# A rearranged opening of a hybrid encoder layer, with 27 products of a constant on TensorE

## The chip, the cores and the metric

The kernel runs on one core of a Trainium2 chip. The metric is the device time of one execution in microseconds; a kernel is given by the median of its runs. The engines of the core are called PE (TensorE, matrix products), DVE (VectorE), ACT (ScalarE), POOL (GpSimd) and SP (SyncE, which here issues the DMAs). A core has one queue of instructions for each engine; they meet only at semaphores. SBUF holds 128 partitions, and products are written to eight banks of PSUM.

## What is computed

One layer of a streaming encoder, in float32, for a prompt of 1024 frames and a sample of 64 frames, so 1088 token rows of width 1024:

```python
def _rmsnorm(x, g):
    y = x * lax.rsqrt(jnp.mean(x * x, axis=-1, keepdims=True) + EPS)
    return y * g

def _swiglu_half(x, g, w_gate, w_up, w_down):        # w_gate, w_up: 1024 x 2816
    h = _rmsnorm(x, g)
    return 0.5 * ((jax.nn.silu(h @ w_gate) * (h @ w_up)) @ w_down)

x = x + _swiglu_half(x, g_ffn1, w1_gate, w1_up, w1_down)
x = x + mix(x)                  # attention and mLSTM heads, in and out projections
x = x + _swiglu_half(x, g_ffn2, w2_gate, w2_up, w2_down)
x = _rmsnorm(x, g_final)
```

The change lies in the first 40 us or so, in the norm of the first `_swiglu_half` and in the first of its gate and up products.

## The kernel before

**Precision and products.** A float32 product is made of three passes (`three_pass`, lines 291 to 293): each operand is split into a high part (ACT copies it to a rounded type) and a low part (a subtraction, operand less its high part), and TensorE sums high x low, high x high and low x high. The up and gate products of the FFN go in pairs of 128-column tiles of the weights, 11 pairs in all; from the second pair on, the pair is done with seven products in place of eight (Strassen's scheme), on sums of operand quarters. The first pair, "the opening", is done directly, as 16 chains of 24 products with 272 columns each (`start_chain`), a chain for each matrix (gate, then up), token half j, and quarter i.

**The opening.** x comes in nine blocks of 128 rows (the ninth, block 8, has the 64 rows of the sample) by DMA to XIN. For each block TensorE transposes eight squares into two banks (line 845), and DVE (line 856) or ACT (line 851) copies the two banks to X. ACT squares the rows with an accumulated sum (line 862) and takes roots in groups of blocks (`GROUP`, line 869); DVE makes reciprocals (line 874) and diagonal matrices of them (line 877); TensorE multiplies ONES with these diagonals (line 888, `start_roots`, n = 0 to 3), which puts 1/rms of every token into a bank across all partitions. DVE scales X with it and with the gain (line 935, `start_scale`), ACT makes the high part (line 946), DVE the low part (line 950). The four weight quarters of the gate and the four of the up matrix get their high parts on ACT (line 961) and their low parts on DVE (line 965).

**The second token half and the spill.** The unscaled X is needed later for the residual, so SP writes it to DRAM as soon as all of it has been copied out of PSUM (`xsp`, line 465, four DMAs: two for the first half of the tokens, then two for the second half). The scale of the first half writes to a buffer of its own (HJ); the scale of the second half writes in place into X and therefore waits until the DMA of that part has landed. The wait of SP before the second pair of DMAs is `sp.wait_ge(x_evA, 10)`: ACT's tenth copy, which is the second bank of block 8.

**What sets the order.** Everything around the change is written out by hand, one list of calls for each engine: `start_pe_tokens`, `start_pe_pair`, `start_act_tokens`, `start_dve_tokens`. An engine goes through its list and stands still at a wait that isn't fulfilled. Behind the opening, `start_difference` and `start_feature` steps (lines 1020, 1035, 1042) make the operand sums of the token quarters for the seven products, and `up` steps make those of the weights: sums on GpSimd (lines 556, 558, 559, 566), high parts on ACT (line 578), low parts on DVE (line 583); lines 703, 765 and 768 add up products on DVE and GpSimd.

## Time and profile before

| what | value |
|---|---|
| time, median of 3 runs | 1945.61 us (1944.47 to 1946.06) |
| the profiled execution | 1945.54 us, of which the span of the trace 1944.0 us |
| mean granted TensorE clock in it | 0.998 |
| TensorE busy | 1924.2 us (99%) |
| VectorE, ScalarE, GpSimd busy | 66%, 40%, 54% |
| DMA, mean | 151 GB/s |

Where a row of a timeline has "x4", four instructions one behind the other are joined, and the duration is that of all; the bracket at the end says how long the engine was idle before, and who ended that idle time.

### The profile page before, as it was taken

What the parts mean: (1) busy time and instruction counts of PE and PEld (TensorE: products, weight loads), DVE (VectorE), ACT (ScalarE), POOL (GpSimd) and SP (SyncE); (2) the same over time, 40 slices, a digit from 0 to 9 for tenths busy, and PEclk for the clock granted to TensorE, in tenths of its full rate; (3) what the DMA queues carried; (4) which work ended last, traced back from release to release, by engine and by line L of the source; (5) the groups of instructions that cost most, each with busy time, mean ns of one, the idle gap of its engine ahead of it and who ended that gap; (6) DMA issues with size and microseconds to landing.
All of it is one profiled execution on the core that took longest, in us unless ns stands there. A gap on an engine that the chain in (4) does not pass through costs nothing.

```text
span 1944.0 us, 39225 instructions
## 1 busy us (share of the span) xinstructions
PE 1924.2 (99%) x14627; PEld 1882.3 (97%) x14627; DVE 1284.3 (66%) x1882; ACT 783.4 (40%) x1595; POOL 1053.3 (54%) x958
## 2 busy tenths in 40 slices
PE   8999999999999999999999999999999999999998
PEld 7999999999999999999998999999999999999997
DVE  6866777666566788864445664866767667656674
ACT  6433333333443345733334542443333333344343
POOL 2277776775777641321222442237767776686770
PEclk9999999999999999999999999999999999999999
DMA  8135445334986530342332834214454444498552
GB/s 271 46 114 178 140 162 179 132 132 156 316 311 188 169 102 14 116 119 90 100 104 62 207 94 124 79 56 145 150 180 144 132 154 164 151 362 276 165 157 104
DMA packets 226846, 293.88 MB, mean 151 GB/s; under 512 B 16616, under 2 KB 158472, under 8 KB 226736
## 3 DMA queue, kind: packets, MB, share of 16 engines
q1 hardware_dynamic: 219040, 272.76, 43.8%
q0 software_dynamic: 7696, 19.63, 3.2%
q8 instruction: 71, 1.16, 0.3%
q14 instruction: 39, 0.32, 0.1%
HBM read 198.07 MB, written 94.21 MB: 150 GB/s over the span
## 4 chain that ended last, share of the span: by engine, by line
PE 96%; DVE 1%; DMA 1%; issue 1%; POOL 1%; ACT 0%; SPq 0%; ACTq 0%; POOLq 0%
PE bank L291 29%; PE bank L292 29%; PE bank L293 29%; PE bank L2583 1%; PE bank L2602 1%; PE bank L2593 1%; DMA XIN<-in_x_prompt 1%; PE bank L2514 0%; PE bank L1332 0%; PE bank L1334 0%; PE bank L1333 0%; PE bank L1328 0%; PE bank L845 0%; PE bank L2694 0%; PE bank L2692 0%
## 5 line engine op out<-in xcount | busy, mean ns | idle before, releaser
L291 PE MATMUL bank<-HA,HW 128*128 128x272 f32 x1120 | 322.7, 288 | 0.0
L292 PE MATMUL bank<-HA,HW 128*128 128x272 f32 x1120 | 322.3, 288 | 0.0
L293 PE MATMUL bank<-HA,HW 128*128 128x272 f32 x1120 | 322.1, 288 | 0.0
L1381 DVE SCALAR_TENSOR_TENSOR HW<-WRAW,HW 128x512 fp32r<-128x512 f32 x140 | 224.5, 1644 | 103.8 <-ACT HW L1376 103.3
L1387 POOL TENSOR_TENSOR HA<-ARAW,HA 128x544 fp32r<-128x544 f32 x140 | 222.6, 1607 | 101.8 <-ACT HA L1375 101.6
L291 PE MATMUL bank<-HL,WGH 128*128 128x368 f32 (+2 forms) x784 | 255.6, 326 | 0.0
L293 PE MATMUL bank<-HH,WGL 128*128 128x368 f32 (+2 forms) x784 | 246.3, 314 | 1.1 <-issue 1.1
L292 PE MATMUL bank<-HH,WGH 128*128 128x368 f32 (+2 forms) x784 | 246.2, 314 | 0.0
L292 PE MATMUL bank<-FC,WR 128*128 128x272 f32 x768 | 222.1, 289 | 0.0
L291 PE MATMUL bank<-FC,WR 128*128 128x272 f32 x768 | 220.4, 287 | 0.6 <-DVE WR L583 0.5
L293 PE MATMUL bank<-FC,WR 128*128 128x272 f32 x768 | 220.1, 287 | 0.0
L292 PEld LDWEIGHTS bank<-HA,HW 128*128 128x128 f32 x1120 | 211.1, 189 | 0.0
L293 PEld LDWEIGHTS bank<-HA,HW 128*128 128x128 f32 x1120 | 211.1, 189 | 0.0
L291 PEld LDWEIGHTS bank<-HA,HW 128*128 128x128 f32 x1120 | 210.5, 188 | 0.2 <-POOL HA L1387 0.2
L814 POOL TENSOR_TENSOR SA<-SA,PV 128x272 f32<-128x272 f32 x160 | 140.4, 898 | 101.3 <-DVE PV L703 98.1
L583 DVE TENSOR_TENSOR WR<-RAWU,WR 128x512 fp32r<-128x512 f32 x100 | 99.3, 993 | 134.3 <-ACT WR L578 134.3
L1375 ACT ACTIVATE HA<-ARAW 128x544 fp32r<-128x544 f32 x140 | 91.6, 654 | 232.3 <-PE bank L293 163.5
L629 ACT ACTIVATE SA<-SA 128x272 f32<-128x272 f32 x160 | 67.5, 431 | 265.9 <-POOL SA L768 137.0
L703 DVE TENSOR_TENSOR PV<-bank,PV 128x272 f32<-128x272 f32 x280 | 118.5, 435 | 77.6 <-POOL PV L765 38.5
L291 PEld LDWEIGHTS bank<-HL,WGH 128*128 128x128 f32 x784 | 147.3, 188 | 14.6 <-issue 12.9
L292 PEld LDWEIGHTS bank<-HH,WGH 128*128 128x128 f32 x784 | 147.5, 188 | 1.6
L293 PEld LDWEIGHTS bank<-HH,WGL 128*128 128x128 f32 x784 | 147.4, 188 | 1.0 <-issue 1.0
(384 smaller groups left out, 5670.6 us busy)
## 6 DMA issues: line engine op xcount, KB each, us to landing
asp<-SA SPq DMA_DIRECT2D x44, 544.0 KB, 3.5
RAWG<-in_w_gate SPq DMA_DIRECT2D x22, 1024.0 KB, 6.5
RAWU<-in_w_up SPq DMA_DIRECT2D x22, 1024.0 KB, 6.4
tsp<-TT SPq DMA_DIRECT2D x40, 544.0 KB, 6.6
ARAW<-tsp SPq DMA_DIRECT2D x80, 272.0 KB, 3.4
WS<-in_w_down SPq DMA_DIRECT2D x20, 1024.0 KB, 8.6
wsp<-WS SPq DMA_DIRECT2D x20, 1024.0 KB, 8.6
WRAW<-wsp SPq DMA_DIRECT2D x80, 256.0 KB, 4.3
```

The source lines that it names most:

```text
L291: nc.tensor.matmul(bank[:, 0:w], w_hi, rhs_lo, start=first, stop=False)
L292: nc.tensor.matmul(bank[:, 0:w], w_hi, rhs_hi, start=False, stop=False)
L293: return nc.tensor.matmul(bank[:, 0:w], w_lo, rhs_hi, start=False, stop=last)
L583: nc.vector.tensor_tensor(WR[:, o, 1], weight(o, q0, mat), WR[:, o, 0].bitcast(F32), ALU.subtract).then_inc(s_.lo, 1)
L629: nc.scalar.activation(tile, tile, ACT.Silu).then_inc(s_.silu, 1)
L703: nc.vector.tensor_tensor(out, bank, add, ALU.add).then_inc(s_.ev, 1)
L814: nc.gpsimd.tensor_tensor(gated(j, slot), gated(j, slot), PV[j][:, tile], ALU.mult).then_inc(s_.mul, 1)
L1375: nc.scalar.activation(HA[f][h][:, 0], ARAW[r][:, :, :], ACT.Copy).then_inc(down_hi, 1)
L1381: nc.vector.scalar_tensor_tensor(out=HW[f][h][:, 1], in0=WRAW[r][:, :], scalar=0.5, in1=HW[f][h][:, 0].bitcast(F32), op0=ALU.mult, op1=ALU ...
L1387: nc.gpsimd.tensor_tensor(HA[f][h][:, 1], ARAW[r][:, :, :], HA[f][h][:, 0].bitcast(F32), ALU.subtract).then_inc(down_alo, 1)
L2583: mm = nc.tensor.matmul(BANK[2 + i // 2][:, (i % 2) * 256:(i % 2) * 256 + 256], QB[rows, par, 2 * g_ + hl // 2, :], KW[rows, par, 0 if g_ ...
L2593: tr = nc.tensor.transpose(BANK[4 + w][:, i * P:(i + 1) * P], SP[:, i, w * P:(w + 1) * P], IDENT[:, :])
```

## The change

It rewrites the four lists of the opening and what hangs on their counts.

- GpSimd makes ONES first, then issues the DMA of the gain and makes the other constants. Behind its constants it computes the low parts of the eight weight quarters (`start_weight_low_pool`), which DVE did.
- TensorE waits for ONES alone, multiplies ONES by ONES 8 times into bank 7, which nothing reads, and then for the other constants. Five such products stand between the transposes of block 1 and block 2, three ahead of the first roots and eleven behind them, 27 in all (`start_idle`). Only blocks 0 to 4 are transposed ahead of the first chain (before: 0 to 5); block 5 and the second roots follow behind it, and the third and fourth roots one chain later than before.
- The roots come in five groups (before: four), blocks 0 and 1 apart from block 2; all later counts of the semaphores follow (`ROOTS`).
- DVE copies blocks 0, 1, the first bank of 2, then 3 and 4; ACT the second bank of 2, then 5 to 8. So ACT makes 9 copies and DVE 9.
- ACT's list: weight quarters 4 to 7 and the squares of blocks 5, 6 and 7 stand ahead of the copy of block 8.
- The banks of the opening's chains rotate over six banks instead of using four; a chain waits for whoever last used its bank (`start_bank_free`). A chain of the first token half waits for the low parts of its two weight quarters one by one.
- SP's wait ahead of the spill of the second half is again for the second bank of block 8 (now ACT's ninth copy).

```diff
-        GROUP = ((0, 3, P), (3, 5, P), (5, 8, P), (8, 9, DEC))
+        GROUP = ((0, 2, P), (2, 3, P), (3, 5, P), (5, 8, P), (8, 9, DEC))
+        ROOTS = len(GROUP)
...
             elif j:
-                sp.wait_ge(x_evA, 10)
+                sp.wait_ge(x_evA, 9)
             else:
-                sp.wait_ge(x_evV, 8)
-                sp.wait_ge(x_evA, 4)
+                sp.wait_ge(x_evV, 9)
+                sp.wait_ge(x_evA, 1)
...
-        BLOCK_BANK = (0, 2, 4, 6, 2, 0, 6, 2, 6)
+        BLOCK_BANK = (0, 2, 4, 6, 2, 6, 2, 6, 6)
...
+        def start_weight_low_pool(pool, i):
+            pool.wait_ge(st.whi, i + 1)
+            nc.gpsimd.tensor_tensor(WR[:, i, 1], first_weight(i), WR[:, i, 0].bitcast(F32), ALU.subtract).then_inc(st.wlo, 1)
...
+        def start_bank(f, mat, j, i):
+            return BANK[i if f else (8 * j + 4 * mat + i) % 6]
...
         def start_chain(pe, f, mat, j, i, between=None):
             fh, th = (i // 2, i % 2) if mat and j else (i % 2, i // 2)
             if j == 0:
-                pe.wait_ge(st.wlo, 8 * f + 4 * mat + 2 * fh + 2)
-            if mat:
+                pe.wait_ge(st.wlo, 8 * f + 4 * mat + 2 * fh + (2 if f else 1))
+            if f == 0:
+                start_bank_free(pe, mat, j, i)
+            elif mat:
...
             for kh in range(2):
                 e = 2 * th + kh
+                if f == 0 and j == 0 and kh:
+                    pe.wait_ge(st.wlo, 4 * mat + 2 * fh + 2)
...
+        def start_idle(pe, count):
+            for _ in range(count):
+                nc.tensor.matmul(BANK[7][:, 0:P], ONES[:, :], ONES[:, :], start=True, stop=True)
+
         def start_pe_tokens(pe):
-            for b in range(3):
-                start_transpose(pe, b)
+            pe.wait_ge(const_ops, 1)
+            start_idle(pe, 8)
+            pe.wait_ge(const_ops, 7)
+            start_transpose(pe, 0)
+            start_transpose(pe, 1)
+            start_idle(pe, 5)
+            start_transpose(pe, 2)
+            start_idle(pe, 3)
             start_roots(pe, 0)
-            for b in range(3, 6):
-                start_transpose(pe, b)
-            start_roots(pe, 1)
+            start_idle(pe, 11)
+            start_transpose(pe, 3)
+            start_transpose(pe, 4)
...
                 start_chain(pe, f, 0, 0, 0)
+                start_transpose(pe, 5)
+                start_roots(pe, 1)
                 start_transpose(pe, 6)
+                start_chain(pe, f, 0, 0, 1)
                 start_transpose(pe, 7)
-                start_chain(pe, f, 0, 0, 1)
+                start_chain(pe, f, 0, 0, 2)
                 start_transpose(pe, 8)
-                start_chain(pe, f, 0, 0, 2)
-                start_chain(pe, f, 0, 0, 3, between=lambda: start_roots(pe, 2))
+                start_chain(pe, f, 0, 0, 3)
+                start_chain(pe, f, 1, 0, 0, between=lambda: start_roots(pe, 2))
                 start_roots(pe, 3)
...
+            for i in range(8):
+                start_weight_low_pool(pool, i)
             up_pool(pool, 0)
```

**ACT, between the weight quarters 2 and 3 and the end of its list.** The names: XIN is x as loaded, X x transposed, HJ x scaled, FC and FBa operands of the products, WR the split weights, RAWG and RAWU the loaded ones, JK and SSB squares and their sums, RMB roots, DG diagonals. L961 are weight high parts, L851 copies from PSUM (4x128: a bank of a full block; 4x64: a bank of block 8), L946 high parts of the scaled x, L862 squares, L869 (L867 now) roots. Before:

```order
L862 ACTIVATE JK,SSB<-XIN_78 128x1024
L851 ACTIVATE X<-bank 128x4x128 x2
L946 ACTIVATE FBa<-HJ_65 128x4x272
L851 ACTIVATE X<-bank 128x4x128 x2
L946 ACTIVATE FC<-HJ_65 128x4x272
L961 ACTIVATE WR<-RAWU 128x512 x2
L862 ACTIVATE JK,SSB<-XIN_78 128x1024 x2
L869 ACTIVATE RMB<-SSB,GQOE 128x3
L851 ACTIVATE X<-bank 128x4x64 x2
```

The same place of ACT's queue after the change:

```order
L851 ACTIVATE X<-bank 128x4x128 x4
L946 ACTIVATE FBa<-HJ_65 128x4x272
L946 ACTIVATE FC<-HJ_65 128x4x272
L851 ACTIVATE X<-bank 128x4x128 x2
L961 ACTIVATE WR<-RAWU 128x512 x4
L862 ACTIVATE JK,SSB<-XIN_78 128x1024 x3
L867 ACTIVATE RMB<-SSB,GQOE 128x3
L851 ACTIVATE X<-bank 128x4x64 x2
```

Between the copy of block 7 and that of block 8 (4x64) now stand four weight high parts, three squares and a root; before, one x high part, two weight high parts, two squares and a root stood there.

**DVE, from the first diagonals to the second scale.** L856 are copies from PSUM, L874 (L872 now) reciprocals, L877 (L875) diagonals, L935 scales, L950 low parts of x, L965 low parts of the weights. Before:

```order
L856 COPY X<-bank 128x4x128 x6
L874 RECIPROCAL RMB<-RMB 128x3
L877 TENSOR_SCALAR DG<-IDENT,RMB 128x128 x3
L935 SCALAR_TENSOR_TENSOR HJ_65<-X,GC,bank 128x272 x8
L950 TENSOR_TENSOR FC<-HJ_65,FC 128x4x272
L874 RECIPROCAL RMB<-RMB 128x2
L877 TENSOR_SCALAR DG<-IDENT,RMB 128x128 x2
L965 TENSOR_TENSOR WR<-RAWG,WR 128x512 x2
L950 TENSOR_TENSOR FBa<-HJ_65,FBa 128x4x272
```

DVE's queue at that place after the change:

```order
L856 COPY X<-bank 128x4x128
L872 RECIPROCAL RMB<-RMB 128x1
L875 TENSOR_SCALAR DG<-IDENT,RMB 128x128
L935 SCALAR_TENSOR_TENSOR HJ_65<-X,GC,bank 128x272 x8
L950 TENSOR_TENSOR FC<-HJ_65,FC 128x4x272
L950 TENSOR_TENSOR FBa<-HJ_65,FBa 128x4x272
L856 COPY X<-bank 128x4x128 x2
```

The weight low parts are gone from DVE, one copy and one diagonal stand between block 2's first bank and the first scale instead of two copies and three diagonals, and the two low parts of x follow one another.

## Rows read from the trace of the kernel before

**Rows 1.** The page's first part: busy time, share of the span, instructions.
```profile
PE 1924.2 (99%) x14627; PEld 1882.3 (97%) x14627; DVE 1284.3 (66%) x1882; ACT 783.4 (40%) x1595; POOL 1053.3 (54%) x958
```

**Rows 2.** TensorE's waits, 0 to 110 us: total us, times, longest.
```profile
PE bank L845 <- POOL BD L1699: 5.1, 1, 5.1
...
PE bank L291 <- DVE WR L583: 0.5, 1, 0.5
```

**Rows 3.** Timeline of TensorE, opening: start, duration, operation, [idle before <-releaser].
```profile
5.05 3.65 PE L845 MATMUL bank<-IDENT,XIN 128*128 128x128 f32 x16 [5.05 <-POOL BD L1699]
...
12.12 0.84 PE L888 MATMUL bank<-DG,ONES 128*128 128x128 f32 x6 [1.74 <-DVE DG L877]
14.61 5.38 PE L845 MATMUL bank<-IDENT,XIN 128*128 128x128 f32 x24 [1.65 <-DMA XIN<-in_x_prompt]
...
20.73 0.36 PE L291 MATMUL bank<-FC,WR 128*128 128x272 f32 x1
...
21.94 0.28 PE L291 MATMUL bank<-FC,WR 128*128 128x272 f32 x1
```

**Rows 4.** Timeline of DVE, 40 to 102 us.
```profile
40.95 1.72 DVE L935 SCALAR_TENSOR_TENSOR X<-X,GC,bank 128x272 f32<-128x272 f32 x4 [1.96 <-DMA xsp<-X]
...
65.91 2.25 DVE L583 TENSOR_TENSOR WR<-SS,WR 128x512 fp32r<-128x512 f32 x2
...
72.99 1.28 DVE L583 TENSOR_TENSOR WR<-RAWG,WR 128x512 fp32r<-128x512 f32 x2
...
74.54 1.43 DVE L583 TENSOR_TENSOR WR<-RAWG,WR 128x512 fp32r<-128x512 f32 x1
...
76.42 1.65 DVE L1042 TENSOR_TENSOR FBa<-TS,FBa 128x1088 fp32r<-128x1088 f32 x1
78.11 2.26 DVE L1020 TENSOR_TENSOR TS<-X,TS 128x1088 f32<-128x1088 f32 x1
...
100.45 1.39 DVE L583 TENSOR_TENSOR WR<-RAWU,WR 128x512 fp32r<-128x512 f32 x1 [1.02 <-ACT WR L578]
```

**Rows 5.** The waits of SP's queue, 0 to 60 us: total us, times, longest.
```profile
SPq L465 <- ACT X L851: 9.3, 1, 9.3
```

**Rows 6.** Timeline of ACT, 26 to 33 us.
```profile
26.41 1.09 ACT L851 ACTIVATE X<-bank 128x512 f32<-128x512 f32 x2
27.36 1.14 ACT L946 ACTIVATE FC<-HJ 128x1088 fp32r<-128x1088 f32 x1
28.37 1.17 ACT L961 ACTIVATE WR<-RAWU 128x512 fp32r<-128x512 f32 x2
29.41 1.08 ACT L862 ACTIVATE JK<-XIN 128x1024 f32<-128x1024 f32 x1
...
31.85 0.30 ACT L869 ACTIVATE RMB<-SSB,GQOE 128x3 f32<-128x3 f32 x1
32.05 0.64 ACT L851 ACTIVATE X<-bank 128x256 f32<-128x256 f32 x2
```

**Rows 7.** Windows: stretch, length, busy time of each engine, PEclk, DMA share, GB/s.
```profile
14.00:16.00 2.00, 1.39 (x7) 1.39 (x8) 2.00 (x6) 2.00 (x5) 0.00 (x0) 0.50 1.09 352
...
20.00:22.00 2.00, 1.87 (x16) 1.79 (x16) 2.00 (x4) 1.97 (x4) 0.00 (x0) 1.00 1.13 226
```

**Rows 8.** Timeline of DVE, 9 to 19 us.
```profile
9.98 1.29 DVE L856 COPY X<-bank 128x512 f32<-128x512 f32 x2 [0.55 <-PE bank L845]
...
11.39 0.68 DVE L877 TENSOR_SCALAR DG<-IDENT,RMB 128x128 f32<-128x128 f32 x3
13.07 3.36 DVE L935 SCALAR_TENSOR_TENSOR HJ<-X,GC,bank 128x272 f32<-128x272 f32 x8 [1.00 <-issue]
16.77 1.29 DVE L950 TENSOR_TENSOR FC<-HJ,FC 128x1088 fp32r<-128x1088 f32 x1 [0.34 <-ACT FC L946]
```

**Rows 9.** Timeline of POOL (GpSimd), 60 to 80 us.
```profile
65.72 1.28 POOL L566 TENSOR_TENSOR RAWG<-RAWG,SS 128x512 f32<-128x512 f32 x1 [16.30 <-DVE WR L583]
73.18 2.24 POOL L556 TENSOR_TENSOR SS<-RAWU 128x512 f32<-128x512 f32 x1 [6.17 <-PE bank L293]
```

More of the change, by code:

```diff
@@ L838, in start_transpose @@
             pe.wait_ge(block_in[b], 16)
[L839 to L842 removed]
+            if b in (4, 5, 6):
+                pe.wait_ge(x_evV, {4: 4, 5: 7, 6: 9}[b])
+            elif b in (7, 8):
+                pe.wait_ge(x_evA, {7: 3, 8: 7}[b])
             for half in range(2):
@@ L846, in start_transpose, with start_evict_act, start_evict_dve @@
                 tr.then_inc(x_tr, 1)
-        def start_evict_act(act, b):
-            for half in range(2):
+        def start_evict_act(act, b, halves=(0, 1)):
+            for half in halves:
                 act.wait_ge(x_tr, 2 * b + half + 1)
                 nc.scalar.activation(X[:, 4 * half:4 * half + 4, b * P:b * P + (P if b < NB else DEC)], block_banks(b, half), ACT.Copy).then_inc(x_evA, 1)
-        def start_evict_dve(dve, b):
-            for half in range(2):
+        def start_evict_dve(dve, b, halves=(0, 1)):
+            for half in halves:
                 dve.wait_ge(x_tr, 2 * b + half + 1)
@@ L882, in start_roots @@
             if n == 0:
-                pe.wait_ge(x_evV, 6)
-            elif n == 2:
-                pe.wait_ge(x_evA, 10)
+                pe.wait_ge(x_evV, 5)
+            elif n == 1:
+                pe.wait_ge(x_evA, 1)
+            else:
+                pe.wait_ge(x_evA, 9)
             for b, c0, c1 in pieces(n):
@@ L965, in start_weight_low, with start_bank_free @@
             nc.vector.tensor_tensor(WR[:, i, 1], first_weight(i), WR[:, i, 0].bitcast(F32), ALU.subtract).then_inc(st.wlo, 1)
+        def start_bank(f, mat, j, i):
+            return BANK[i if f else (8 * j + 4 * mat + i) % 6]
+        def start_bank_free(pe, mat, j, i):
+            q = 8 * j + 4 * mat + i
+            if q < 2:
+                pe.wait_ge(x_evV, 2)
+            elif q < 4:
+                pe.wait_ge(x_evA, 5)
+            elif q < 6:
+                pe.wait_ge(st.ht, 2 * i + 2)
+            elif q in (10, 11, 12, 13):
+                pe.wait_ge(st.mul, q - 9)
+            else:
+                pe.wait_ge(st.silu, {6: 1, 7: 2, 8: 3, 9: 4, 14: 5, 15: 6}[q])
         def start_chain(pe, f, mat, j, i, between=None):
@@ L994, in start_silu @@
             act.wait_ge(st.pm, 16 * f + 8 * j + i + 1)
-            nc.scalar.activation(gated(j, i % 2 * 2 + i // 2), BANK[i][:, 0:HT], ACT.Silu).then_inc(st.silu, 1)
+            nc.scalar.activation(gated(j, i % 2 * 2 + i // 2), start_bank(f, 0, j, i)[:, 0:HT], ACT.Silu).then_inc(st.silu, 1)
         def start_gate(dve, f, j, i):
@@ L1072, in start_act_tokens @@
         def start_act_tokens(act):
-            for b in range(3):
-                start_block_square(act, b)
+            start_block_square(act, 0)
+            start_block_square(act, 1)
             start_block_root(act, 0)
+            start_block_square(act, 2)
+            start_block_root(act, 1)
+            start_evict_act(act, 2, (1,))
+            start_high(act, 0, 0, 0)
             start_weight_high(act, 0, 0)
+            start_high(act, 0, 0, 1)
             start_weight_high(act, 0, 1)
             start_block_square(act, 3)
-            start_high(act, 0, 0, 0)
             start_block_square(act, 4)
-            start_block_root(act, 1)
-            start_high(act, 0, 0, 1)
-            start_evict_act(act, 5)
-            start_evict_act(act, 3)
+            start_block_root(act, 2)
             start_weight_high(act, 0, 2)
             start_weight_high(act, 0, 3)
-            start_block_square(act, 5)
+            start_evict_act(act, 5)
             start_evict_act(act, 6)
             start_high(act, 0, 0, 2)
+            start_high(act, 0, 0, 3)
             start_evict_act(act, 7)
-            start_high(act, 0, 0, 3)
-            start_weight_high(act, 0, 4)
-            start_weight_high(act, 0, 5)
-            start_block_square(act, 6)
-            start_block_square(act, 7)
-            start_block_root(act, 2)
+            for i in range(4, 8):
+                start_weight_high(act, 0, i)
+            for b in (5, 6, 7):
+                start_block_square(act, b)
+            start_block_root(act, 3)
             start_evict_act(act, 8)
             start_block_square(act, 8)
-            start_block_root(act, 3)
-            start_weight_high(act, 0, 6)
-            start_weight_high(act, 0, 7)
+            start_block_root(act, 4)
         def start_act_features(act):
@@ L1136, in start_dve_tokens @@
         def start_dve_tokens(dve):
-            for b in range(3):
-                start_evict_dve(dve, b)
+            start_evict_dve(dve, 0)
+            start_evict_dve(dve, 1)
             start_diagonals(dve, 0)
+            start_evict_dve(dve, 2, (0,))
+            start_diagonals(dve, 1)
             start_scale(dve, 0, 0, 0, 0)
@@ L1679, in _ @@
         def _(pool):
+            nc.gpsimd.memset(ONES[:, :], 1.0).then_inc(const_ops, 1)
             pool.dma_start(GC[:, 0, :], a["g_ffn1"][0].rearrange("(k p) -> p k", p=P)).then_inc(gain_in, 16)
             nc.gpsimd.memset(IDENT[:, :], 0.0).then_inc(const_ops, 1)
-            nc.gpsimd.memset(ONES[:, :], 1.0).then_inc(const_ops, 1)
             nc.gpsimd.memset(BD[:, :], 0.0).then_inc(const_ops, 1)
```

60 lines of the change are left out of this document (22 added, 38 removed).

## The prediction

> **What bounds the kernel now.** I read the page's busy shares first. TensorE is busy 99% of the span [rows 1], so a microsecond is won or lost only where TensorE waits. Next came the view of what each engine waited for, for TensorE in the first 110 us: 5.1 us until the constants (the row names the last of them) and the first block of x are there, others among the transposes, and then one single wait of 0.5 us, for a DVE subtract of the up weights, in the first Strassen pair [rows 2]. Between the first real matmul at 20.73 [rows 3] and that wait at 101.9, TensorE never stands still. That looks as if the opening were paid only by TensorE. It is not so, and this is the point of the forecast.
>
> Follow the wait backwards on DVE. The subtract that TensorE waited for is the one that starts at 100.45. From there back to 40.95, no DVE row has an idle time that TensorE ended: DVE is full, or waits for ACT or GpSimd, which wait for DVE in turn. The start of this run of work is the scale of the second token half, in place in X, at 40.95, and what it waited for is the landing of the copy of X to DRAM [rows 4]. That copy may only be issued when the last block of x has been copied out of PSUM: SyncE sat 9.3 us until an ACT copy of X [rows 5], the 256-element copy of block 8 at 32.05, which ended at 32.69 [rows 6]. So the time to about 102 us is set by this chain: **ACT's copy of block 8, the spill, DVE's 60 us of operands**, and TensorE's 0.5 us wait shows that TensorE is just ahead of it. Whatever moves block 8's copy moves the end; what makes TensorE start earlier in the opening only lengthens the wait at 102.
>
> **The idle matmuls and the early constant.** The constant's memset moves ahead of one DMA issue and one memset on GpSimd, and the first idle matmuls run before 5.05, when TensorE has nothing [rows 3]. I cost both at nothing; the 5.05 us wait for x covers them. The first broadcast, 272 columns, took 0.84 us [rows 3], so a 128-column product of the same constant is at most 0.84 x 128 / 272 = 0.4 us. Five of them ahead of block 2 are 2.0 us at most. In the old trace the first 16 transposes took 3.65 us, 0.23 each, and the 24 at 14.61 also 0.22 each, in a stretch whose granted clock is 0.50 [rows 3, 7]; so the first ones ran at the lower level (1.2 GHz) as well. If the idle work lifts the clock for them, they are limited by the arrival of block 1, end about 1.7 us earlier, near 7.0, and the five idle ones end at 9.0. Block 2 is there by then and not much sooner: DVE could copy its first half at 9.98 [rows 8], four transposes of 0.23 after 9.06. Eleven behind the broadcast fill the gap to block 3 at 14.61. Without the lift the cover is gone; that is a rival below.
>
> **The first scale** comes earlier. Between the first half of block 2 and the broadcast, DVE had two copies (1.29), a reciprocal and three diagonals (0.68), 9.98 to 12.07, or 2.09 together [rows 8]. Now one copy (half of 1.29), the reciprocal (the 0.12 between) and one diagonal (0.23) stand there, 1.0: the second half goes to ACT, which has time then. The scale starts at 13.07 - 1.1 = 12.0 and ends at 12.0 + 3.36 = 15.4 [rows 8].
>
> **The weight subtracts** go from DVE to GpSimd. DVE saves eight. On GpSimd a subtract of that size took 1.28 us [rows 9]. The first weight is split by ACT after the first activation: 13.7 + 1.1 + 0.6 = 15.4; the second after the second activation: 15.4 + 1.1 + 0.55 = 17.0. Were GpSimd undisturbed, its second subtract would end at 18.3. But in the same 15.4 to 18 DVE now has two subtracts of 1088 columns, 1.29 each [rows 8], with both operands in SBUF. The trace has this case. DVE's pair of 512-column subtracts took 1.28 at 72.99 but 2.25 at 65.91 [rows 4], where GpSimd's 1.28 at 65.72 lay beside it [rows 9]; and the GpSimd sum at 73.18 took 2.24 [rows 9], while DVE's operations at 74.54, 76.42 and 78.11 took 1.43, 1.65 and 2.26 instead of 0.64, 1.29 and 1.29 [rows 4, 8]. The one waits until the other is done. The four operations then come one behind the other: 15.4 + 2 x 1.29 + 2 x 1.28 = 20.5. I take this end, since four rows of the same shapes show it; the other end is 18.3.
>
> (The Trainium skill, GPSIMD Engine Reference, § 1 Specifications, says that GpSimd's SBUF interface is shared with VectorE, and that a VectorE instruction with two SBUF inputs contends. This speaks against moving the subtracts here, and the rows at 65.72 and 65.91 agree with it: 0.97 us more on DVE. By the rule the second subtract ends at 20.5, without it at 18.3, and the sum below is 3.2 or 1.0.)
>
> **From the second subtract to block 8's copy.** The second half of chain 0 needs it: its 12 products, at nine steps from 20.73 to 21.94 [rows 3], are 1.6, so chain 0 ends at 22.1. Only behind it stand block 5's transposes, 0.9 (a third of 5.38, halved for the full clock, which the rows from 20 on show [rows 3, 7]), and the second broadcast with its step to DVE, 0.95 as at 12.12 to 13.07 [rows 3, 8]: the second scale starts at 23.95 and, at 3.36 as the first, ends at 27.3. Then comes ACT's queue, in the new order, where I use the distance from one start to the next in its old rows [rows 6]: activation of the last quarter 1.0, block 7's copies 0.95, four weight splits 2.1 (2 x 1.04), three squares 3.65 (two from 29.41 to 31.85), a root 0.2, block 8's copy 0.64. That sums to 8.55, so the copy ends at 27.3 + 8.55 = 35.85, say 35.9. **It ended at 32.69, so the spill goes out 3.2 us later.** Before, two of those weight splits stood behind the copy, and the last three squares were partly done earlier.
>
> **The sum.** Behind the spill the work is what it was: same landing (issued with the same reload traffic behind it), same DVE and ACT operations. The scale starts at 40.95 + 3.2 = 44.15, the subtract of the up weights ends 3.2 later, and TensorE's wait of 0.5 grows by that and by its own lead. The rest of the 1945.54 profiled us is TensorE's. 1945.54 + 3.2 = **1948.7 us**. The profiled execution and the median of the three runs (1945.61) differ by 0.07, nothing beside the bounds. If the chain came earlier instead, no more than 0.5 us could be won up to 102.
>
> **Rivals.** (a) *The engines do not hold each other up here.* The subtracts end at 18.3, everything from the second half of chain 0 on comes 2.2 us earlier, the shift is 1.0: 1946.5. For it: the operations may interleave otherwise than at 65.72. Against: all rows of like shapes.
> (b) *The opening order does what its start promises*: ACT reaches block 8's copy no later than before, since it takes its squares in gaps that I gave to waiting. Then the old 0.5 us wait is all that can move: 1945.0 to 1945.5. Against: ACT has 2.3 us more of weight splits ahead of the copy than before, whatever the gaps.
> (c) **Slower by more:** *GpSimd's three sums fall differently.* They are released by TensorE (6.17 us idle before 73.18, ended by a TensorE bank [rows 9]), which is about 1 us ahead, while DVE's chain is 3.2 behind; so they lie some 4 us earlier against DVE's work, on operand subtracts. Three sums are 3.9 us; DVE paid 0.75 + 0.36 + 0.97 = 2.1 for them [rows 4]. If it pays all three in full: 1.8 more, 1950.5. It decides from 0.7 us more than forecast. Against: a part of the sums may as well fall on rows where DVE waits for ACT, and then the price falls by as much.
> (d) *The idle matmuls do not do what they say*: the clock stays at 1.2 GHz. Then the first transposes end at 8.7, five idle products 2.0 later, block 2's first four transposes end at 11.6, the scale starts at 13.9 instead of 12.0, and all behind it shifts by 1.9: 1950.6. In the old trace the clock was at 0.50 from 14 to 16, behind a gap that TensorE spent waiting (1.74 and 1.65 us ahead of 12.12 and 14.61 [rows 3]), and at 1.00 from 20 [rows 7], after the transposes had filled it; idle work in just those gaps speaks against this.
>
> **How the numbers follow.** Forecast 0.35, (a) 0.2, (b) 0.13, (c) 0.21, (d) 0.08, and 0.03 for something that gains by a way I don't see. A difference under 0.2%, 3.9 us, can hardly be told from no change here: the bounds are 1941.7 and 1949.5. Forecast, (a) and (b) lie inside, (c) and (d) outside; of the forecast a small part, 0.03, lies beyond the bound. Faster 0.03, same 0.65, slower 0.32. The range reaches from the middle of (b), 1945.2, to beyond (c), 1951.0, which leaves out about 0.07 + 0.03 below and 0.06 above.
>
> **What will show it.** Right: block 8's copy ends near 35.9 on ACT; DVE's scale after the spill starts near 44.2; the single TensorE wait before 110 us for an up-weight subtract has grown to some 4 us or has split into several; the first subtracts on GpSimd or DVE's beside them are longer than 1.29. Wrong: a copy of block 8 at 33 or earlier, or TensorE dense to 102 although the scale is late. The granted clock from 12 to 20 at 1.00 would show the idle work's effect, and a first chain that still waits for its weights shows that it wins nothing by it.

## The result and the profile after the change

The changed kernel takes 1948.78 us (median of 16 runs, 1947.8 to 1951.17) against 1945.08 for the kernel before, measured with it (16 runs): a ratio of 1.0021, with a 95% interval of 1.0014 to 1.0028. It is slower by about 4 us (3.7 between the medians), and 1948.7 was forecast. The profiled execution took 1947.88 (span 1946.3), near the lowest of the 16.

What TensorE waited for between its first chain and 112 us (total, times, longest), where before it was 0.5 us for an up-weight subtract [rows 2]:

```profile
PE bank L291 <- DVE SA L1023: 3.9, 1, 3.9
```

One wait of 3.9 us, eight times the old one, but for another instruction: the product of gate and up (L1023, L1002 before), the third of the opening's second token half. It reads the bank which TensorE's third Strassen product writes next; until then that product waits.

The timeline of ACT, where the chain was expected to be late (start, duration, operation, [idle before <-releaser]); it answers to [rows 6]:

```profile
26.40 1.12 ACT L946 ACTIVATE FC<-HJ 128x1088 fp32r<-128x1088 f32 x1 [0.52 <-DVE HJ L935]
27.42 1.07 ACT L851 ACTIVATE X<-bank 128x512 f32<-128x512 f32 x2
28.37 2.19 ACT L961 ACTIVATE WR<-RAWU 128x512 fp32r<-128x512 f32 x4
30.45 1.05 ACT L862 ACTIVATE JK<-XIN 128x1024 f32<-128x1024 f32 x1
...
34.32 0.64 ACT L851 ACTIVATE X<-bank 128x256 f32<-128x256 f32 x2
```

The last high part, block 7's copies, four weight splits, three squares (the first at 30.45), a root, and only then block 8's copy, which ends at 34.96: 2.27 us later than before. In these two profiles the whole delay arises here: ACT begins this stretch at 26.40, as it did before (26.41, there with block 7's copies [rows 6]), and the stretch has two weight splits more (1.04) and one square more (1.24). Then DVE, in the opening (answering to [rows 8]) and behind the spill (to [rows 4]):

```profile
12.02 3.36 DVE L935 SCALAR_TENSOR_TENSOR HJ<-X,GC,bank 128x272 f32<-128x272 f32 x8 [1.01 <-PE bank L888]
...
16.55 2.12 DVE L950 TENSOR_TENSOR FBa<-HJ,FBa 128x1088 fp32r<-128x1088 f32 x1
...
23.01 3.36 DVE L935 SCALAR_TENSOR_TENSOR HJ<-X,GC,bank 128x272 f32<-128x272 f32 x8 [1.35 <-ACT X L851]
...
43.23 1.78 DVE L935 SCALAR_TENSOR_TENSOR X<-X,GC,bank 128x272 f32<-128x272 f32 x4 [2.03 <-DMA xsp<-X]
...
46.48 2.17 DVE L950 TENSOR_TENSOR FBa<-X,FBa 128x1088 fp32r<-128x1088 f32 x1
...
72.56 2.33 DVE L1041 TENSOR_TENSOR TS<-X,TS 128x1088 f32<-128x1088 f32 x1
74.81 1.58 DVE L585 TENSOR_TENSOR WR<-RAWG,WR 128x512 fp32r<-128x512 f32 x1
76.32 2.35 DVE L1041 TENSOR_TENSOR TS<-X 128x1088 f32<-128x1088 f32 x1
78.59 0.42 DVE L1023 TENSOR_TENSOR SA<-SA,bank 128x272 f32<-128x272 f32 x1
...
104.12 1.39 DVE L585 TENSOR_TENSOR WR<-RAWU,WR 128x512 fp32r<-128x512 f32 x1 [1.02 <-ACT WR L580]
```

The scale behind the spill starts at 43.23 instead of 40.95 (+2.28), the up-weight subtract at 104.12 instead of 100.45 (+3.67). In between, four operations are 0.9 to 1.1 us longer than their like: 46.48 (2.17 for 1.28), 72.56, 74.81 (1.58 for 0.68) and 76.32, the last three directly ahead of the product at 78.59 that TensorE waits for. GpSimd shows why (answering to [rows 9]):

```profile
15.49 4.13 POOL L965 TENSOR_TENSOR WR<-RAWG,WR 128x512 fp32r<-128x512 f32 x2 [3.04 <-ACT WR L961]
...
47.57 2.22 POOL L560 TENSOR_TENSOR SS<-SS,RAWG 128x512 f32<-128x512 f32 x1
...
72.44 1.30 POOL L558 TENSOR_TENSOR SS<-RAWU 128x512 f32<-128x512 f32 x1 [2.51 <-PE bank L293]
73.82 2.02 POOL L560 TENSOR_TENSOR SS<-SS,RAWU 128x512 f32<-128x512 f32 x1
75.81 1.71 POOL L561 TENSOR_TENSOR RAWU<-RAWU 128x512 f32<-128x512 f32 x1
```

Its sums of the gate weights lie beside 46.48, and its three sums of the up weights, released by TensorE at 72.44 (73.18 before) and done at 77.5, beside the three operations from 72.56 to 78.6; e4 below tests this. Before, DVE had reached the third product by then, and the sums fell on what came behind it. Its row in DVE's timeline of the kernel before:

```profile
72.64 0.42 DVE L1002 TENSOR_TENSOR SA<-SA,bank 128x272 f32<-128x272 f32 x1
```

The wait has a second price. Windows of one microsecond (stretch, length, busy time of each engine, granted clock, DMA share, GB/s) just behind it:

```profile
79.00:80.00 1.00, 0.84 (x5) 0.88 (x6) 1.00 (x3) 0.81 (x1) 0.00 (x0) 0.70 0.00 0
80.00:81.00 1.00, 1.00 (x6) 1.00 (x6) 1.00 (x3) 0.00 (x0) 0.00 (x0) 0.50 0.00 0
81.00:82.00 1.00, 1.00 (x6) 1.00 (x5) 1.00 (x3) 0.00 (x0) 0.00 (x0) 0.50 0.51 196
82.00:83.00 1.00, 1.00 (x7) 1.00 (x6) 0.97 (x2) 0.40 (x1) 0.00 (x0) 0.59 1.02 292
```

TensorE, idle from 75.29 to 79.16, runs at half clock until about 82.8; 0.30, 0.50, 0.50 and 0.41 are missing from the four windows' clocks, 1.7 us of work. In the opening, on the other hand, the clock, 0.50 from 14 to 16 before [rows 7], is 1.00, and the first chain starts at 17.88 instead of 20.73 [rows 3]. Most of the earlier start is the new order's: e3 below, the changed kernel without the products, has it at 17.72, and runs with them at 17.2 to 17.9.

TensorE's timeline of the changed kernel:

```profile
17.88 0.37 PE L291 MATMUL bank<-FC,WR 128*128 128x272 f32 x1
```

Windows (stretch, length, busy time of each engine, granted clock, DMA share, GB/s) of the changed kernel:

```profile
14.00:16.00 2.00, 1.55 (x13) 1.12 (x11) 2.00 (x5) 2.00 (x3) 0.51 (x1) 1.00 0.98 320
```

How far TensorE is behind in all shows in the first gate subtract for the pair after, which waits for ACT and this for TensorE's products. That row in DVE's timeline of the kernel before:

```profile
107.62 0.69 DVE L583 TENSOR_TENSOR WR<-RAWG,WR 128x512 fp32r<-128x512 f32 x1 [0.88 <-ACT WR L578]
```

The same row after the change:

```profile
111.80 0.86 DVE L585 TENSOR_TENSOR WR<-RAWG,WR 128x512 fp32r<-128x512 f32 x1 [1.43 <-ACT WR L580]
```

4.18 us: the wait of 3.87 and 1.7 of missing clock, less the old wait of 0.47, less the 0.74 by which TensorE had been ahead (72.44 for 73.18) come to 4.36, which is 0.2 too much. Behind it the two kernels do the same. (The two profiled runs end only 2.34 us apart. 1.1 us of the rest is a stop of TensorE near 1184 us, which only the profile before has; some 0.7 more lies far behind the change and is not explained.)

### The profile page after: what moved, and what is told of

Its sections match the earlier page's. It is cut to its first block, busy times and chain, and to the rows that moved or that the text cites. A ratio compares the mean times of both kernels' runs of the same rounds, so it can differ in the third digit from the quotient of the medians.

```text
span 1946.3 us, 39342 instructions
## 1 busy us (share of the span) xinstructions
PE 1929.3 (99%) x14681; PEld 1886.7 (97%) x14681; DVE 1281.6 (66%) x1876; ACT 783.6 (40%) x1595; POOL 1060.2 (54%) x966
## 4 chain that ended last, share of the span: by engine, by line
PE 93%; DVE 3%; DMA 1%; ACT 1%; POOL 1%; issue 1%; SPq 0%; DVEq 0%; ACTq 0%; POOLq 0%
PE bank L291 29%; PE bank L292 29%; PE bank L293 28%; PE bank L2613 1%; PE bank L2632 1%; PE bank L2623 1%; DVE TS L1041 1%; PE bank L2544 0%; PE bank L1362 0%; PE bank L1363 0%; PE bank L1364 0%; PE bank L1358 0%; PE bank L2724 0%; DMA xsp<-X 0%; PE bank L2722 0%
```

## The experiments

Theory: the end is set by block 8's copy, through the spill and DVE's in-order queue. Rivals: the weight subtracts on GpSimd, the new order on TensorE, and the idle products. Ratios are to the kernel before on the same chip, with 95% intervals; "gate subtract" is the row that stood at 107.62 before.

| run | edit | block 8's copy ends | scale behind the spill | up-weight subtract | gate subtract | ratio |
|---|---|---|---|---|---|---|
| before | | 32.69 | 40.95 | 100.45 | 107.62 | |
| after | | 34.96 | 43.23 | 104.12 | 111.80 | 1.0021 (1.0014 to 1.0028) |
| e1 | after, copy earlier | 31.81 | 40.11 | 99.48 | 106.66 | 0.9997 (0.9988 to 1.0006) |
| e2 | before, spill later | 32.32 | 43.03 | 102.79 | 109.97 | 1.0021 (1.0012 to 1.0030) |
| e3 | after, no idle products | 36.45 | 45.64 | 105.60 | 113.08 | 1.0037 (1.0023 to 1.0051) |
| e4 | after, sums later | 34.36 | 42.65 | 101.97 | 109.16 | 1.0012 (1.0003 to 1.0021) |
| e5 | after, lows on DVE | 35.15 | 44.02 | 104.51 | 112.20 | 1.0024 (1.0014 to 1.0035) |
| e6 | after, clock held | 34.37 | 42.66 | 103.55 | 110.72 | 1.0015 (1.0006 to 1.0024) |
| e7 | after, copy behind block 7 | 28.45 | 38.1 | 98.55 | 105.74 | 0.9990 (0.9981 to 0.9999) |
| e8 | before, copy earlier | 29.75 | 38.13 | 99.47 | 106.66 | 0.9995 (0.9986 to 1.0004) |
| e9 | before, idle products | 32.46 | 40.75 | 100.06 | 107.24 | 0.9994 (0.9985 to 1.0003) |
| e10 | e7 without them | 29.76 | 39.2 | 99.51 | 106.69 | 1.0004 (0.9995 to 1.0013) |

Rows of two runs also differ by up to 0.7 us because x lands that much sooner or later. In e7 and e10 the scale is the second half of a joined row of eight.

**e1: the copy of block 8 alone moved forward in the changed kernel.**

```diff
-            for b in (5, 6, 7):
-                start_block_square(act, b)
-            start_block_root(act, 3)
-            start_evict_act(act, 8)
+            start_block_square(act, 5)
+            start_evict_act(act, 8)
+            for b in (6, 7):
+                start_block_square(act, b)
+            start_block_root(act, 3)
             start_block_square(act, 8)
```

> The changed kernel with one edit: ACT copies block 8 right behind the square of block 5, ahead of the squares of 6 and 7 and of a root. If the place of this copy sets the time (copy, spill, DVE's in-order queue), the copy ends near 32.3 us instead of 34.96, DVE's first scale behind the spill's second landing starts near 40.6 instead of 43.23, the third gate product on DVE comes near 73 instead of 78.59, TensorE's wait of 3.9 us at 79.16 and the 3.4 us of half clock behind it go, and a wait of 0.5 to 2.3 us for an up-weight subtract near 102 is left: 1945.4 us, some 3.4 below the changed kernel. If instead the subtracts on GpSimd or the new order on TensorE cost the time, it stays within 1 us of the changed kernel, 1948 to 1949.5.

1943.51 us where the kernel before has 1944.26, a little better than the expected time. One line of ACT's list takes the whole loss back. ACT's and DVE's timelines and TensorE's waits to 112 us:

ACT's timeline of e1:

```profile
31.16 0.65 ACT L851 ACTIVATE X<-bank 128x256 f32<-128x256 f32 x2
```

DVE's timeline of e1:

```profile
40.11 1.78 DVE L935 SCALAR_TENSOR_TENSOR X<-X,GC,bank 128x272 f32<-128x272 f32 x4 [1.77 <-DMA xsp<-X]
...
71.65 0.42 DVE L1023 TENSOR_TENSOR SA<-SA,bank 128x272 f32<-128x272 f32 x1
```

TensorE's waits from 24 to 112 us (total, times, longest) of e1:

```profile
PE bank L291 <- DVE WR L585: 0.6, 1, 0.6
```

The third product is at 71.65, as early as before, the wait for it is gone, and a wait of 0.6 for the up-weight subtract is back, as in the kernel before. The idle products, the new order and the subtracts on GpSimd are all still there; none of them by itself makes the loss.

**e2: the late spill alone, in the kernel before.** SP also waits for ACT's last weight high part, which in the profile before ended 2.35 us behind block 8's copy; nothing else changes.

```diff
             elif j:
                 sp.wait_ge(x_evA, 10)
+                sp.wait_ge(st.whi, 8)
```

> The kernel before with one edit: SyncE's spill of the second token half also waits for ACT's last weight high part (near 35.05 us), so it goes out some 2.35 us later; nothing else is changed. If the spill's time sets the end, DVE's scale moves from 40.95 to about 43.3, GpSimd's three up-weight sums, released by TensorE at 73.2, fall on the subtracts ahead of the third gate product, TensorE waits 2 to 3 us for that product near 76 and runs at half clock for a while behind it: 1948 us (1947.2 to 1949). If what costs is the opening's new order on TensorE, DVE and GpSimd, which this kernel doesn't have, it stays at 1945.

1947.76 us against 1944.26, ratio 1.0021, the same as that of the whole change. DVE's timeline and TensorE's waits:

DVE's timeline of e2:

```profile
43.03 1.72 DVE L936 SCALAR_TENSOR_TENSOR X<-X,GC,bank 128x272 f32<-128x272 f32 x4 [2.03 <-DMA xsp<-X]
...
73.33 2.37 DVE L1021 TENSOR_TENSOR TS<-X 128x1088 f32<-128x1088 f32 x1
75.62 0.42 DVE L1003 TENSOR_TENSOR SA<-SA,bank 128x272 f32<-128x272 f32 x1
```

TensorE's waits from 24 to 112 us (total, times, longest) of e2:

```profile
PE bank L291 <- DVE SA L1003: 2.0, 2, 1.4
PE bank L291 <- DVE WR L584: 0.7, 1, 0.7
```

The spill is issued at 34.80 instead of 32.72. It makes waits of the same kind, here in three pieces (2.0 in two, and 0.7 for the up-weight subtract). The half clock that was expected behind them is not in this profile, where the granted clock is 1.00 from 74 to 82; its gate subtract is 2.35 late, and the run is the fastest of eleven (1945.49 to 1949.59). e1 and e2 together settle the cause: without the late spill there is no loss, and the late spill alone makes one as large, by the ratios.

**e3: the changed kernel without the 27 products** (the four calls of `start_idle` taken out).

> The changed kernel without the 27 products of the constant; all else stays. If the idle products only hold the clock, the granted clock falls to 0.50 somewhere between 12 and 20 us, block 2's transposes and chain 0's first half take longer, the second scale and with it block 8's copy come 0 to 1 us later, and the time is 1948.8 to 1950.3, most likely 1949.3. If the idle products themselves delay the chain (three and eleven stand ahead of the first broadcast and of block 3), it is faster than the changed kernel by up to 0.5 us.

1951.4 us (five runs) against 1944.26; more than expected. The copy of block 8, the first scale, the first chain and the clock of the opening:

ACT's timeline of e3:

```profile
35.81 0.64 ACT L851 ACTIVATE X<-bank 128x256 f32<-128x256 f32 x2
```

DVE's timeline of e3:

```profile
11.97 3.36 DVE L935 SCALAR_TENSOR_TENSOR HJ<-X,GC,bank 128x272 f32<-128x272 f32 x8 [1.01 <-PE bank L888]
```

TensorE's timeline of e3:

```profile
17.72 0.57 PE L291 MATMUL bank<-FC,WR 128*128 128x272 f32 x1
```

Windows (stretch, length, busy time of each engine, granted clock, DMA share, GB/s) of e3:

```profile
16.00:18.00 2.00, 1.90 (x9) 1.90 (x10) 2.00 (x2) 2.00 (x4) 2.00 (x2) 0.50 1.05 407
```

TensorE's wait for the third product is 3.9 us as in the changed kernel. The first scale starts as early as with the products, and the first chain within the range of the runs with them (17.2 to 17.9). But without them the clock is 0.50 while the first chain runs, and block 5, which is transposed behind that chain, the second scale and block 8's copy come 1.5 us later (36.45 against 34.96). In the new order the idle products are worth 1.5 us at block 8's copy, 1.3 at the gate subtract and about 3 by the ratios, whose intervals overlap a little (1.0023 and 1.0028). They are a part of the change that helps.

**e4: the sums of the up weights on GpSimd held back**, so that they don't lie beside the operations ahead of the third product.

```diff
             if first and mat:
-                pool.wait_ge(st.pm, 16 * f + 16)
+                pool.wait_ge(st.mul, 8 * f + 8)
```

> The changed kernel with one edit: GpSimd's three sums of the up weights wait for DVE's eighth gate product instead of TensorE's sixteenth chain, so they no longer lie beside the subtracts ahead of the third gate product (2.33, 1.58 and 2.35 us instead of 1.28, 0.68 and 1.28). The third gate product then comes near 75.6, TensorE's wait at 79.16 shrinks from 3.9 to 1 us or less and the clock holds. If DVE's run from the spill to the up-weight subtract sets the end, the wait comes back as one of 3 to 4 us near 105 for that subtract and the time stays within 1 us of the changed kernel: 1948.2. If the collision alone is the cost, the time falls by 3 to 5 us: 1944 to 1946.

1946.27 against 1944.26: between the two theories' numbers. DVE's timeline and TensorE's waits:

DVE's timeline of e4:

```profile
73.74 1.28 DVE L1041 TENSOR_TENSOR TS<-X 128x1088 f32<-128x1088 f32 x1
74.94 0.42 DVE L1023 TENSOR_TENSOR SA<-SA,bank 128x272 f32<-128x272 f32 x1
...
101.97 1.38 DVE L585 TENSOR_TENSOR WR<-RAWU,WR 128x512 fp32r<-128x512 f32 x1 [1.02 <-ACT WR L580]
```

TensorE's waits from 24 to 112 us (total, times, longest) of e4:

```profile
PE bank L291 <- DVE WR L585: 1.9, 2, 1.0
PE bank L291 <- DVE SA L1023: 0.8, 1, 0.8
```

The operations have their normal length again, the third product is at 74.94, the wait for it is 0.8, the clock holds, and 1.9 us of waits come back at the up-weight subtracts, as DVE's late start wants it. So of the loss, something like 2.3 us (the ratio 1.0012) is the late start alone, and some 1.8 us is the collision with the clock that it costs. The split is rough, since the intervals of the two ratios overlap. DVE paid 1.5 for the sums here (two operations of 2.0 instead of 1.3), not 3.

**e5: the eight weight subtracts back on DVE.**

```diff
-            for i in range(8):
-                start_weight_low_pool(pool, i)
...
             start_low(dve, 0, 0, 0)
+            start_weight_low(dve, 0, 0)
             start_low(dve, 0, 0, 1)
+            start_weight_low(dve, 0, 1)
...
+            start_weight_low(dve, 0, 2)
+            start_weight_low(dve, 0, 3)
...
+            for i in range(4, 8):
+                start_weight_low(dve, 0, i)
```

> The changed kernel with the eight low parts of the weights back on DVE (0.65 us each, between its other steps); GpSimd has none. In the changed kernel the first two took GpSimd 4.13 us instead of 2 x 1.28, and DVE's second low part of x 2.12 instead of 1.28; here the second one should be done near 19.0 instead of 19.6. If the hand-over of the two engines is the main cost of the change, block 8's copy and all behind it come 1.5 to 2.2 us earlier: 1946.8. If it is a small one, as the 0.6 us between the two ends says, block 8's copy ends at 34.4 instead of 34.96 and the time is 0.3 to 0.8 us below the changed kernel: 1948.2.

1948.73 against 1944.52, neither of the two numbers. Nothing is won; block 8's copy ends at 35.15. The second subtract starts at 18.41 on DVE and ends at 19.1 (on GpSimd it ended at 19.62):

```profile
18.41 0.69 DVE L969 TENSOR_TENSOR WR<-RAWG,WR 128x512 fp32r<-128x512 f32 x1
...
22.01 1.28 DVE L969 TENSOR_TENSOR WR<-RAWG,WR 128x512 fp32r<-128x512 f32 x2
23.21 3.35 DVE L935 SCALAR_TENSOR_TENSOR HJ<-X,GC,bank 128x272 f32<-128x272 f32 x8
```

But DVE is then busy without a gap, the next two subtracts (22.01) stand ahead of the second scale, and that starts at 23.21 (23.01 in the changed kernel), although ACT's copy of block 5, for which it waited there, is done at 22.5: what was won is lost. The engines do hold each other up in the changed kernel (4.13 us for two subtracts), yet the end is no later than with all of it on DVE.

**e6: the clock held through the wait**, by 14 more products of the constant ahead of the product that waited.

```diff
             for o in range(PRODUCTS):
+                if first and f == 0 and mat == 0 and j == 0 and o == 2:
+                    start_idle(pe, 14)
```

> The changed kernel with 14 more products of the constant on TensorE, ahead of the product that waited 3.87 us at 79.16 (they fill about 3.4 us of it). Expected: the granted clock stays at 1.00 through 80 to 83 us, where the changed kernel ran 3.4 us at 0.50 and lost some 1.6. If DVE's run to the up-weight subtract caps the time, TensorE then waits about 1.1 us for that subtract near 105.5 and only 0.5 us is won: 1948.3. If the clock was a cost of its own, all 1.6 us are won: 1947.2.

1947.46 against 1944.52. TensorE's waits, and the clock where it had been 0.50:

TensorE's waits from 24 to 112 us (total, times, longest) of e6:

```profile
PE bank L291 <- DVE SA L1025: 0.7, 1, 0.7
PE bank L291 <- DVE WR L585: 0.7, 1, 0.7
```

Windows (stretch, length, busy time of each engine, granted clock, DMA share, GB/s) of e6:

```profile
80.00:82.00 2.00, 2.00 (x18) 2.00 (x17) 2.00 (x3) 0.40 (x1) 0.00 (x0) 1.00 0.55 185
```

The clock stays at 1.00. The gate subtract stands 1.08 us earlier than in the changed kernel (110.72), 0.6 of which is the earlier landing of x in this run (the scale behind the spill is at 42.66), and a wait of 0.7 for the up-weight subtract is back. So of the 1.7 us of missing clock about 0.5 could be had in this profile, as DVE's cap says; by the ratios (1.0021 and 1.0015) it is 1.2, with intervals that hold both numbers.

**e7: block 8 transposed and copied right behind block 7**, the transposes into banks 4 and 5.

```diff
-        BLOCK_BANK = (0, 2, 4, 6, 2, 6, 2, 6, 6)
+        BLOCK_BANK = (0, 2, 4, 6, 2, 6, 2, 6, 4)
...
-            elif b in (7, 8):
-                pe.wait_ge(x_evA, {7: 3, 8: 7}[b])
+            elif b == 7:
+                pe.wait_ge(x_evA, 3)
+            elif b == 8:
+                pe.wait_ge(st.ht, 4)
...
             elif q < 6:
-                pe.wait_ge(st.ht, 2 * i + 2)
+                pe.wait_ge(x_evA, 9)
...
                 start_transpose(pe, 7)
+                start_transpose(pe, 8)
                 start_chain(pe, f, 0, 0, 2)
-                start_transpose(pe, 8)
...
             start_evict_act(act, 7)
+            start_evict_act(act, 8)
             for i in range(4, 8):
```

> The changed kernel with block 8 transposed right behind block 7 (into banks 4 and 5, once the second scale has read them) and copied by ACT right behind block 7, ahead of the weight splits and the squares. If the place of this copy sets the end, it ends near 29.2 us, DVE's scale behind the spill's last landing starts at 37 to 38, TensorE has no wait over 0.1 us between its first chain and 110 us, and what is left is TensorE's own lead: 1.5 to 2 us less than the kernel before, 1942.5 to 1943.5 where that is at 1944.5. If an earlier spill collides with the loads (the last blocks and the up weights land at 22 to 26 us), it lands no earlier than 39 and the time is that of the run with the copy behind one square, some 0.6 below the kernel before.

1942.14 against 1944.52, ratio 0.9990 (0.9981 to 0.9999): faster than the changed kernel, and than the kernel before by an interval that just leaves out 1. ACT's four copies of blocks 7 and 8, and DVE's eight scales of the third quarter:

ACT's timeline of e7:

```profile
26.83 1.62 ACT L853 ACTIVATE X<-bank 128x512 f32<-128x512 f32 x4
```

DVE's timeline of e7:

```profile
36.28 3.57 DVE L937 SCALAR_TENSOR_TENSOR X<-X,GC,bank 128x272 f32<-128x272 f32 x8
```

The first four scales no longer wait for a landing but follow DVE's diagonals, which wait for ACT's roots; the last four start at 38.1, 0.1 us behind them, when the second transfer has landed. So the spill paces DVE hardly any more. TensorE has no wait between 24 and 112 us. What is won over the kernel before, 1.9 us at the gate subtract, is the old wait and TensorE's lead (GpSimd's sums are released at 71.61 instead of 73.18).

**e8: the same idea in the kernel before**: block 8's copy ahead of two squares and a root.

```diff
+            start_evict_act(act, 8)
             start_block_square(act, 6)
             start_block_square(act, 7)
             start_block_root(act, 2)
-            start_evict_act(act, 8)
```

> The kernel before with one edit: ACT copies block 8 ahead of the squares of blocks 6 and 7 instead of behind them and a root. The copy ends near 30.1 instead of 32.69, DVE's scale behind the spill starts at 38 to 39, and TensorE's single wait of 0.47 us at 101.89 goes; nothing more can be won, since TensorE is dense from 20.73 on: 0.5 us below the kernel before. If TensorE's wait is not tied to the spill, nothing changes. Against the run with the copy behind block 7 in the new order, the difference, 1 to 1.5 us, is what the new order of TensorE and the idle products give once the spill is out of the way.

1943.12 against 1944.52, 0.9995 (0.9986 to 1.0004), not told apart from the kernel before; the gate subtract moved by 0.96. Now DVE waits for TensorE:

ACT's timeline of e8:

```profile
29.10 0.65 ACT L851 ACTIVATE X<-bank 128x256 f32<-128x256 f32 x2
```

DVE's timeline of e8:

```profile
63.87 0.44 DVE L1002 TENSOR_TENSOR SA<-SA,bank 128x272 f32<-128x272 f32 x1 [1.25 <-PE bank L293]
```

The scale is 2.8 us earlier, and the up-weight subtract only 1.0: the product at 63.87 waits 1.25 us for a TensorE bank. From there on TensorE is the bound. Against e7 the gate subtract is 0.92 later, somewhat less than the 1 to 1.5 expected for the new order with its products; by the ratios it is 0.0005, and their intervals overlap.

**e9: only the idle products, in the kernel before.**

```diff
+            nc.gpsimd.memset(ONES[:, :], 1.0).then_inc(const_ops, 1)
             pool.dma_start(GC[:, 0, :], a["g_ffn1"][0] ...
-            nc.gpsimd.memset(ONES[:, :], 1.0).then_inc(const_ops, 1)
...
-            for b in range(3):
-                start_transpose(pe, b)
-            start_roots(pe, 0)
+            pe.wait_ge(const_ops, 1)
+            start_idle(8)
+            pe.wait_ge(const_ops, 7)
+            start_transpose(pe, 0)
+            start_transpose(pe, 1)
+            start_idle(5)
+            start_transpose(pe, 2)
+            start_idle(3)
+            start_roots(pe, 0)
+            start_idle(11)
```

> The kernel before with only the part that the change is named for: ONES made first, and the same 27 products of it at the same places (8 ahead of block 0, 5 and 3 around block 2, 11 ahead of block 3); order, banks and queues stay. Expected: the granted clock is 1.00 through the opening, where the kernel before had 0.50 from 13.07 to 19.90; block 5's transposes end near 18.3 instead of 19.8, and the first chain starts up to 0.7 us earlier, then bound by the low parts of the weights on DVE. If block 8's copy and the spill set the time up to 102 us, nothing is won by that: TensorE's wait of 0.47 at 101.89 grows to about 1 us and the time is that of the kernel before within 0.5 us. If TensorE's start is what counts, it is 0.7 us faster or more.

1944.87 against 1946.38 on this chip, 0.9994 (0.9985 to 1.0003): within 0.2%, and not told apart from nothing. In its profile the clock is 1.00 through the opening, and the first chain waits 0.44 for its weights and starts at 20.06 instead of 20.73; but e2 and e8, which have the old order without the products, start it at 19.96, so that this need not be the products' doing. The wait at the up-weight subtract, expected to grow to about 1 us, is smaller (another 0.4 is spent on an ACT operation, L995):

```profile
PE bank L291 <- DVE WR L583: 0.3, 1, 0.3
```

The gate subtract moves by 0.38, and the scale behind the spill by 0.2.

**e10: e7 without the idle products.**

> The changed kernel with block 8 transposed and copied right behind block 7, without the 27 products. The clock then falls in the opening, as it did without them in the changed kernel (0.50 from 15.29 to 22.11). With the spill out of the way TensorE's own start counts: the first chain is later and partly at half clock, so 1 to 2.5 us are lost against the same kernel with the products (1942.1 where the kernel before has 1944.5): 1943.5 to 1944.5. If the products only mattered through the late spill, the time stays at 1942.1.

1946.72 against 1946.38, 1.0004 (0.9995 to 1.0013), where up to 1 us less than the kernel before was expected. The clock in the opening is back at half:

```profile
18.00:20.00 2.00, 2.00 (x11) 2.00 (x10) 1.96 (x5) 1.88 (x5) 1.58 (x1) 0.52 1.08 315
```

The gate subtract stands 0.95 us behind that of e7; the ratios differ by 0.0014, 2.7 us, with intervals that overlap a little (0.9995 to 0.9999). So once the spill is out of the way the idle products are worth about 1 us in the profiles; that it is more is not shown. The gate subtract stands where it is in e8 (106.69 and 106.66): in the profiles, with the early copy, the new order without the products gives no more than the old one.

## Why the prediction was right, step by step

**The bound** was named rightly: block 8's copy, the spill, DVE's run behind it. e1 takes the loss away by moving that copy alone, e2 makes the same loss by delaying the spill alone.

**The first scale**: 12.0 to 15.4 was forecast, 12.02 to about 15.3 measured. **The idle products** cost nothing and held the clock, as the forecast assumed. But the first scale does not need them: in e3 it starts at 11.97 without them. Rival (d) built its 1950.6 on a first scale at 13.9; e3's 1951.4 is near that number by another way, a first chain at half clock. Nor does the granted clock bear out that the first transposes ran at 1.2 GHz: it is 1.00 up to 12 us in both kernels, though 16 of them took 3.65 us before and 2.22 after.

**The weight subtracts** were the term that was too large: the four operations were to end at 20.5 and ended at 19.62 (15.49 + 4.13), since they overlapped in part. All that follows was therefore 0.9 early: second scale 23.01 for 23.95, block 8's copy 34.96 for 35.9. (What the second scale waited for is ACT's copy of block 5, not the broadcast; the step from chain 0's end was nearly the same, 1.7 for 1.85.) The shift of the spill is 2.27 and not 3.2; the shares behind the subtracts (8.55 us in ACT's queue were forecast, 34.96 - 26.37 = 8.6 measured) were right. Against the kernel before, though, the second scale is not late at all (23.55 there): the whole shift of 2.27 is the two weight splits and the square that the new list puts ahead of the copy, the 2.3 us which the forecast held against rival (b). The two engines do hold each other up at the subtracts: 4.13 us on GpSimd for two, 2.12 on DVE for 1.28. The rule of the Trainium skill (GPSIMD Engine Reference, § 1 Specifications), that a VectorE instruction with two SBUF inputs contends with GpSimd, agrees with these rows. But e5 shows that taking the subtracts back to DVE wins nothing.

**"Behind the spill the work is what it was"** was the step that failed. DVE's queue took 60.9 us from the scale to the up-weight subtract instead of 59.5, because GpSimd's sums fell otherwise: 0.9 us at 46.48 (where 0.3 was paid before), and 3.0 ahead of the third product where 2.1 had been paid behind it. This is rival (c), put at 1.8 more and measured at about 1.4 net, of which 0.9 is the three sums that it named and 0.5 the sums of the gate weights that it did not. The wait is therefore not where it was forecast (the up-weight subtract) but 25 us earlier, and costs half clock besides. The first error and this one are 0.9 too much and 1.4 too little, which makes the up-weight subtract 3.67 late and not 3.2, and the half clock, which the forecast did not have, helps to bring the gate subtract to 4.18. So the 3.2 came near the 3.7 of the medians partly by luck. That the bound stands without the luck is what e1 and e2 show; e4 shows the collision.

**Still open:** the profiles and the medians don't agree to the last microsecond. e2's gate subtract is 2.35 us late in its profile, and its median 3.5; the runs of one kernel spread over 2.5 to 5 us, a profile is one of them, and whether the clock behind the waits differs between them stays open.

## What to carry to other kernels

An engine that is busy for 99% of the span may still be paced by another: look for the first operation of the other's run that has a DMA as its releaser, and ask what lets that DMA go. A short copy that opens a transfer belongs near the head of its queue; here 0.6 us of ACT's work stood behind 6 us of splits, squares and a root. Ahead of two squares and the root (e1) it gave back some 4.7 us of 1949 by the ratios, ahead of all of it (e7) some 6. And an engine that becomes earlier can make another later: GpSimd's sums, released by a TensorE that was ahead, fell on a DVE that was behind.

## What the runs showed of the hardware

A wait of 3.87 us on TensorE cost another 1.7 by the clock that was granted behind it (0.50 for some 3.4 us); in e6 14 products of a constant in that wait kept it at 1.00. Operations with two inputs in SBUF, one on DVE and one on GpSimd, lengthened each other: 128x1088 on DVE took 1.28 us alone and up to 2.35 in the changed kernel beside GpSimd's 128x512, which took 1.29 alone and up to 2.22 beside DVE's (e4 has the same DVE operations without GpSimd's, at 1.28). The clock came back while TensorE did nothing but float32 transposes: in e8 these run from 14.39 to 19.15, and the granted clock goes from 0.50 to 1.00 between 18 and 19. And an earlier spill doesn't always land earlier: its second transfer, issued at 28.9 in e7 and at 30.2 in e8, took 9.1 and 7.8 us to land, so that both landed at 38.0.
